# Seven gate matmuls per recurrence step instead of six, and four instead of five per pair of attention steps

## What is computed

```
h = RMSNorm(x)
a_q, a_k, a_v, i_q, i_k, i_w, b_q, b_f, b_i, b_g, c_q, gates = split(h @ w_in)
y_a = sparse attention: an indexer picks keys, then softmax over them     # 6 heads of 128
y_b = HGRN2 gated recurrence over b_q, b_f, b_i, read out with b_g         # 6 heads
y_c = attention into 256 memory tokens                                     # 4 heads
merged = sig(g_a)*(y_a @ w_out_a) + sig(g_b)*(y_b @ w_out_b) + sig(g_c)*(y_c @ w_out_c)
x = x + RMSNorm(merged @ w_out)
x = x + RMSNorm((relu(RMSNorm(x) @ w_up))**2 @ w_down)
```

## Time and profile before

| | |
|---|---|
| median of 3 runs | 2363.96 us (2361.92 to 2364.99) |
| profiled execution, its own time | 2359.06 us |
| its span in the trace | 2357.3 us |
| PE busy in the span | 2272.2 us (96%) |
| PEld busy in the span | 2118.2 us (90%) |
| DVE, ACT, POOL busy | 1215.5, 714.3, 652.8 us |
| mean granted clock of PE | 0.988 |

### The profile page before, as it was taken

How to read it: one execution, slowest core, us unless ns; L and a number is a source line. 1 busy time by engine, 2 the same in 40 slices (tenths; PEclk the granted TensorE clock), 3 DMA queues, 4 the chain that set the end, 5 groups by cost and what they waited for, 6 DMA issues and landing times. The chain is left out here.

```text
span 2357.3 us, 40632 instructions
## 1 busy us (share of the span) xinstructions
PE 2272.2 (96%) x16446; PEld 2118.2 (90%) x16446; DVE 1215.5 (52%) x2112; ACT 714.3 (30%) x1483; POOL 652.8 (28%) x742
## 2 busy tenths in 40 slices
PE   6989999999999899889999999979999999999998
PEld 6989999999999788778878999979889899898896
DVE  4125599999990577155543655163333233233335
ACT  5224412212121244445544423252112122121222
POOL 3453531212321688200001212151121212121215
PEclk9999999999999999999999999989999999999999
DMA  5342222323233544522216633140201102012014
GB/s 168 111 118 75 67 85 81 102 84 102 84 102 121 168 140 113 173 81 85 59 40 201 187 117 110 49 143 19 72 18 53 54 18 70 18 53 71 18 54 160
DMA packets 210564, 214.54 MB, mean 91 GB/s; under 512 B 33776, under 2 KB 191792, under 8 KB 210416
## 3 DMA queue, kind: packets, MB, share of 16 engines
q1 hardware_dynamic: 210416, 212.49, 28.9%
HBM read 153.03 MB, written 59.43 MB: 90 GB/s over the span
## 5 line engine op out<-in xcount | busy, mean ns | idle before, releaser
L264 POOL TENSOR_TENSOR w_lo<-w_raw,w_hi 128x2048 fp32r<-128x2048 f32 (+2 forms) x41 | 174.3, 4252 | 617.3 <-ACT w_hi L257 617.3
L2516 POOL TENSOR_TENSOR w_lo<-w_raw,w_hi 128x2048 fp32r<-128x2048 f32 x31 | 143.0, 4612 | 580.0 <-ACT w_hi L2547 580.0
L277 PE MATMUL ps<-f_hi,w_hi 128*128 128x384 f32 (+1 forms) x768 | 251.7, 328 | 1.8 <-DVE ff_relu_sq L2585 1.8
L277 PE MATMUL ps<-f_hi,w_lo 128*128 128x384 f32 (+1 forms) x768 | 251.2, 327 | 0.0
L277 PE MATMUL ps<-f_lo,w_hi 128*128 128x384 f32 (+1 forms) x768 | 250.9, 327 | 0.0
L277 PE MATMUL ps<-h_hi,w_lo 128*128 128x384 f32 (+1 forms) x768 | 250.5, 326 | 0.0
L277 PE MATMUL ps<-h_lo,w_hi 128*128 128x384 f32 (+1 forms) x768 | 250.3, 326 | 0.0
L277 PE MATMUL ps<-h_hi,w_hi 128*128 128x384 f32 (+1 forms) x768 | 250.3, 326 | 0.0
L662 ACT ACTIVATE b_stage<-ps 128x256 f32<-128x256 f32 (+5 forms) x203 | 83.5, 414 | 514.9 <-PE ps L277 498.1
L2606 DVE TENSOR_TENSOR big<-big,ps 128x512 f32<-128x512 f32 x144 | 94.8, 658 | 262.4 <-PE ps L277 244.2
L2593 DVE TENSOR_TENSOR ff_relu_sq<-ff_relu_sq 128x384 f32<-128x384 f32 (+1 forms) x96 | 101.1, 1053 | 223.4 <-ACT ff_relu_sq L2556 223.2
(11 more groups left out here) (234 smaller groups left out, 5420.4 us busy)
## 6 DMA issues: line engine op xcount, KB each, us to landing
w_raw<-in_w_in SPq DMA_DIRECT2D x34, 1024.0 KB, 5.6
w_raw<-in_w_up SPq DMA_DIRECT2D x16, 1024.0 KB, 5.6
w_raw<-in_w_down SPq DMA_DIRECT2D x16, 1024.0 KB, 5.4
gm_gate<-d_gate SPq DMA_DIRECT2D x48, 192.0 KB, 2.6
d_gate<-gatef_stage SPq DMA_DIRECT2D x28, 192.0 KB, 2.6
gm_y_raw<-d_y SPq DMA_DIRECT2D x8, 576.0 KB, 4.8
n_x<-in_x_prompt SPq DMA_DIRECT2D x8, 512.0 KB, 7.4
w_raw<-in_w_mem_kv SPq DMA_DIRECT2D x4, 1024.0 KB, 7.4
```

The source lines that it names most:

```text
L264: engine.tensor_tensor(g.w_lo[:, s, 0:size], g.w_raw[:, s, 0:size], g.w_hi[:, s, 0:size].bitcast(F32), ALU.subtract).then_inc(g.w_split, 1)
L277: last = pe.matmul(out, left(a, kk), right(b, kk), start=(kk == 0 and n == 0), stop=(kk == k - 1 and n == 2))
L2516: G.tensor_tensor(g.w_lo[:, slot, :], g.w_raw[:, slot, :], g.w_hi[:, slot, :].bitcast(F32), ALU.subtract).then_inc(g.w_split, 1)
```

## The change

Two tables of numbers. The number of filler matmuls after each tick of the recurrence goes from 6 to 7, and the second group in each attention slot from 3 to 2. The work is the same; 90 filler matmuls stand earlier in PE's list. At the end of the recurrence 678 of 1008 are issued instead of 588, before the first scores 744 instead of 654, and after the last slot 32 are left instead of 64. The evictions, the rounding, the stores, the slab loads and the split pieces move with them in the lists of ACT, SP and POOL. DVE's list is the same.

```diff
-LEAD_IN, PER_TICK = 48, 6
+LEAD_IN, PER_TICK = 48, 7
...
-LEAD_IN_A, PER_TURN, PER_SLOT = 24, 3, (2, 3)
+LEAD_IN_A, PER_TURN, PER_SLOT = 24, 3, (2, 2)
```

## The result

| | before | changed |
|---|---|---|
| median of 20 runs each | 2362.44 us | 2366.74 us |
| span of the profiled execution | 2357.3 us | 2367.3 us |
| ratio, with its 95% interval | | 1.0015 (1.0008 to 1.0022) |

The change makes the kernel about 4 us slower: 4.3 by the medians, 1.9 to 5.2 by the interval of the ratio. By the bound of the prediction (0.2%) that is no change. The forecast was 2368.1 us. One execution of a kernel further down, the one before with its store first, took 7843.8 us; its ratio leaves this execution out.

What follows compares the result with a forecast made beforehand. The prediction took PE to be the bound nearly everywhere, so only its waits could bring gain or loss. Seven terms summed to +4.1 us on a median of 2363.96, giving 2368.1 us, range 2361 to 2373.

Steps and rivals of the forecast that it cites:

- Step 1: Recurrence: 14.9 us of added filler matmuls, of which 1.4 us fall into idle time; +13.5 us.
- Rival (b): Recurrence: the new matmuls find more cover, all 4.9 us; sum +0.6, 2364.6 us; chance 0.12.
- rival (d): Recurrence: PE has room for all the added matmuls, so they cost nothing there; 2354.6 us; chance 0.05.
- Step 2: Turns ahead of the scores: new wait for unit 29's eviction, held by a store queued behind loads; +4.4 us.
- rival (c): Turns: the store does not queue behind the loads and lands early; sum -4.0, 2360.0 us; chance 0.08.
- Step 3: First attention slots: PE should run at 2.4 GHz instead of mostly 1.2 GHz; -2.0 us.
- Rival (a): First scores and merge start: the lower clock follows the new stalls; sum +8.5, 2372.5 us; chance 0.20.
- Step 4: Third tile's slots: the 2.26 us wait behind the last slab's rounding mostly goes; -1.9 us.
- Steps 5 and 6: Attention slots: fewer fillers shorten 32 of 56 slots by 0.16 us, -5.2; evictions move to slot 0, -1.0.
- step 6: Attention slots: evictions fall on slot 0 of each tile, where no turn is waited for; -1.0 us.
- Step 7: Start of the merge: 5.9 us less filler, but PE waits 1.7 us for the first pieces; -3.7 us.

Runs made afterwards that it cites:

- the one before with its store first: Kernel before the change, with the store of filler unit 24 issued ahead of the first load of queries; 2356.79 us, ratio 0.9976 to before.
- the run with evictions in slot 5: Changed kernel with the store of unit 27 ahead of the query loads, and attention lead-in 28 instead of 24 matmuls; 2359.35 us, ratio 0.9985 to before.
- the changed kernel with its store first: Changed kernel with the store of filler unit 27 issued ahead of the first load of queries; 2354.89 us, ratio 0.9968 to before.

## Why the prediction was right

The time came 1.4 us under the forecast. Nearly all of that is the starting point: the forecast added 4.1 us to a median of three runs (2363.96 us), and the median of twenty is 2362.44 us. The difference itself, +4.3 us by the medians against +4.1, agrees more closely than the prediction could claim, and that is luck: its steps miss by up to 0.8 us each, in both directions. But each came in the way that was named and near its size, except for the details said below.

**Step 1, +13.5: right, +14.2.** 14.9 us of matmuls, of which only 0.9 us of waits went (4.75 to 3.82 by the windows), instead of the 1.4 taken. The spot named as free or nearly free, matmul 96, is where the rest stayed: it waited 2.93 us for the eviction of unit 2, the wait of 2.58 us for DVE only changed its name, and the matmuls behind it ran at the lower level as before. ACT's row there, which answers to the earlier trace rows, shows that this eviction waited for a store:

```profile
796.11 0.96 ACT L1062 ACTIVATE gatef_stage<-ps 128x320 f32<-128x320 f32 x2 [13.41 <-DMA d_gate<-gatef_stage]
```

PE went on at 796.59, which is 797.0 on the clock of before (the first step came 0.44 us earlier here), where 795.7 had been taken. The other profiles of these recurrences lie between 195.5 and 196.9 us with 6 per step and between 208.0 and 211.0 with 7, so the term is known to about 2 us. The shortest of the latter is the one in which matmul 96 waited least, 1.29 us, and in which the granted clock did not fall behind it (1.00 over that whole recurrence, against 0.99). Rival (b) would have made it 10.0 us and rival (d) nothing; both are out.

**Step 2, +4.4: right, +5.0, and by the mechanism named, with two misses that cancel in part.** Eviction behind six keys, released by a store, rounding behind it, PE's wait 10.07 us (about 11 forecast). The store landed one microsecond earlier than taken: ACT went on at 1006.26, which is 992.5 on the clock of before, with the first turn as the common point (13.75 us later). The turns after it took 9.95 us instead of 8.3. The four memory turns came as taken, one slow and three fast; but the two key turns and the query turn, for which the earlier trace rows have no row at the lower level, took 1.57, 1.53 and 1.83 us there instead of 1.2, 1.2 and 1.1. The window of that stretch:

```profile
1008.83:1014.67 5.84, 5.49 (x21) 4.47 (x22) 0.00 (x0) 1.75 (x5) 4.71 (x4) 0.50 0.23 78
```

That the queue is the cause, and not a mere coincidence of landing times, is shown by the two kernels that move the store; rival (c) is out. The rule that the prediction set against its own rows (the Trainium skill, "DMA: Bandwidth & Descriptors", section "Queues, rings and completion order": completion is not FIFO per issuing engine) gave no early landing here: the store between the loads landed between them, after 7.1 us.

**Step 3, -2.0: right, a little small.** The granted clock in the first 8 us is 1.00 instead of 0.62; slots 0 to 2 together are 2.7 us shorter (-1.17, -1.94, +0.40). Some 0.5 us of this is not the clock's: with 2 and 2 in the slots alone, which keeps the wait ahead of them, the same slots are 0.5 us shorter, and with 7 per step alone 2.4 us. The granted clock is 1.00 from 1015.29 us on, 3.5 us ahead of the first scores. Rival (a) therefore did not come, although PE stood twice as long: the slow stretch behind the wait fell on turns, not on slots. At the start of the merge, before and changed, the granted clock differs too:

```profile
1251.80:1306.00 54.20, 49.10 (x292) 47.62 (x291) 22.00 (x34) 26.54 (x41) 10.74 (x4) 1.00 0.65 205
```

```profile
1256.30:1310.00 53.70, 49.56 (x285) 48.50 (x286) 21.75 (x33) 25.73 (x40) 10.74 (x4) 0.97 0.74 225
```

The clock of 0.97 instead of 1.00 is worth some 0.03 x 53.7 = 1.6 us. The merge row shows only +0.4, since PE's waits are 1.0 us shorter in this stretch. That the new wait of 1.40 us brought the clock down is not shown: the kernel before with its store first, whose first merge matmul waits for nothing, has 0.97 over the same stretch (1243.96 to 1298.00 us) as well.

**Step 4, -1.9: the wait went, but gave back part; -1.1.** Slot 3 of the third tile went from 5.98 to 4.89 us. The wait of 2.26 us is gone, and behind it three of 0.30, 0.16 and 0.53 us stand in its place: the chain of ACT and DVE sets the end there.

**Steps 5 and 6, -6.2: right, -6.0.** The slots 3 and 5 named as hiding their filler changed by less than 0.3 us, except the one of step 4 and one more (-0.38); slots 0, 1, 2 and 4 from the third tile on are mostly 0.14 to 0.30 us shorter each. The two terms are not told apart by this run. What step 6 put at -1.0 for the evictions was the smallest term and the one least understood: the run with evictions in slot 5 shows that their place is worth 3.25 us of slots, which in this change happens to fall well.

**Step 7, -3.7: right, -4.3 and +0.4.** After the last product 38 matmuls were left, as counted. PE waited 1.40 us where 1.7 were forecast.

The sum of the stages, +5.4, is 1.1 us above the +4.3 of the medians. That is less than single executions differ: the two that were profiled took 2359.06 and 2369.11 us, where the medians are 2362.44 and 2366.74.

## What to carry to other kernels

Filler work in a list that is nearly full is conserved: moving it is worth only the waits that it fills or uncovers, so find the waits first and count matmuls into them, one place at a time. When work moves, follow what moves with it on other engines; here the longer wait for an eviction behind a store in a full DMA queue made 5.0 of the 5.4 us between the profiles, and one store issued ahead of the burst gave back more than twice what the change cost. Halves of a balanced change are not additive, since each alone leaves the next stage with too little or too much cover.

## What was not expected of the hardware

In one profiled execution the granted clock of TensorE fell to 1.2 GHz with almost no idle time recorded ahead of it: in the ninth tile with three fillers per slot, where the steps are only 64 rows wide, the first slots ran at 1.00 with PE busy for 16.84 of 17.00 us, and the rest at 0.52 with PE busy for 19.26 of 19.60 us. With four fillers per slot, in the profile of the changed kernel with its store first, the same tile ran at full clock: the window of all its slots, columns as above, has no low stretch.

```profile
1004.17:1232.87 228.70, 218.12 (x1403) 179.72 (x1403) 124.45 (x398) 115.57 (x310) 2.79 (x4) 1.00 0.23 67
```

The last two slots were 5.9 us longer for it. That the missing fillers brought the clock down is likely, but not shown: the low stretch was seen in one execution, the slowest of ten of that kernel, and what exactly PE did too little of is not told apart by these runs.
